# Moving the down projection's operand and the channel-form operand to other places modulo 512 bytes

## The chip, the core and the metric

The kernel runs on one core of one Trainium2 chip. The metric is the device time of one execution in microseconds (us), lower is better; the median of the runs shown is taken. TensorE (PE) multiplies, its weight loads are listed apart as PEld, VectorE is DVE, ScalarE is ACT, GpSimd is POOL, SyncE is SP.

## What is computed

Twelve layers on 256 tokens of 1024 channels, all in float32: RWKV-7 mixing, attention, two gated short convolutions, a neighbourhood attention, a Hyena mixer, and after each of these six mixers a gated feed-forward network (FFN). Cut to what matters here:

```python
def swiglu(h, w13, w2):                       # the FFN, w2 is the down projection, 2816 x 1024
    g, u = jnp.split(h @ w13, 2, axis=-1)
    return (jax.nn.silu(g) * u) @ w2

def short_conv_mixer(h, w_in, conv_w, w_out): # layers 4 and 10
    b_gate, c_gate, u = jnp.split(h @ w_in, 3, axis=-1)
    return (b_gate * depthwise_conv3(c_gate * u, conv_w)) @ w_out

def hyena_mixer(h, w_in, short_w, ..., w_out): # layer 8
    v, x1, x2 = jnp.split(depthwise_conv3(h @ w_in, short_w, short_b), 3, axis=-1)
    ...                                        # two long convolutions by Fourier transforms
    return z @ w_out

for i in range(DEPTH_2):                       # and a first block of four layers before it
    x = x + mixer(rmsnorm(x, norm_mix_g[i]))
    x = x + swiglu(rmsnorm(x, norm_ffn_g[i]), f_w13[i], f_w2[i])
```

## The kernel before

Every large product is made from three products of rounded numbers. A float32 weight w is split into w_hi (rounded to the type float32r, by ACT, line 1232) and w_lo (the rest, by DVE, line 1666); the activations likewise into a hi and a lo half. `PE_PASSES = ((0, 0), (0, 1), (1, 0))` then gives hi by hi, hi by lo and lo by hi, so three matmuls follow each other for each piece of work, and each loads a stationary operand of its own.

The weights stream in as quarters of 128 x 1024 elements (512 KB) through four slots of `w_raw`, are split into `w_hi` and `w_lo` or, in the layers that have room for them, also into `w_hi_extra` and `w_lo_extra`. A matmul comes in two forms:

- **Token form** (`part_tokens`, line 391; `project`, line 495; `project_part`, line 978): 128 columns of the activations are loaded as the stationary operand, and 512 columns of a weight quarter are streamed past them (the moving operand). The FFN's down projection is `project` on the tiles `hidden_hi` and `hidden_lo` (HH and HL in the code), of 22 blocks of 256 elements a partition.
- **Channel form** (`block_channels`, line 464): 128 columns of a weight quarter are the stationary operand, and the 256 tokens of the activations in `operand_hi` and `operand_lo` (`ah`, `al`) are streamed. It stands in the input projections of the layers 4, 8 and 10 only.

The moving operand of one matmul is read while the stationary operand of the next one is loaded: in the trace of layer 4 the load for the next matmul starts in the same hundredth of a us as the matmul itself.

A place in SBUF is counted in bytes within a partition. From the order of the declarations follow the places of all tiles. Modulo 512, `w_hi`, `w_lo`, `w_hi_extra`, `w_lo_extra`, `operand_hi`, `operand_lo`, `hidden_hi`, `hidden_lo`, `conv_hi` and `conv_lo` all stand at 128 (a tile `align_phases` of 32 bytes sees to that for the last ones), and every block that a matmul takes from them starts a multiple of 512 bytes further on. So with all matmuls of the two forms both operands start at the same place modulo 512; the text calls the difference between them the distance, and it is 0. Two kinds of matmul have another one. In the neighbourhood attention (layer 6) the lines 939 and 941 load `ident_r`, which stands at 256, and stream 256 columns of `bias_hi` or `bias_lo`, at 128: their distance is 128 bytes (float32r, as in the two forms). In layer 0 the line 531 loads columns of `l1_rw` (shown as `l_rw`), whose eight blocks lie 1152 bytes apart, and streams 256 columns of `tmp_rw` blocks 1024 bytes apart: distances of 0, 128, 256 and 384 in turn (plain float32).

ACT writes `operand_hi` (line 1244) and DVE `operand_lo` (line 1687) from PSUM when a layer starts, in four halves of 128 x 512; the channel form's first matmul waits for them. The order of the work is written out by hand, engine by engine. Hyena's own output projection takes `operand_hi` and `operand_lo` too, in token form, after its channel-form products.

Of the kernel before, what the change touches and what calls it, by code (L numbers as in the profile page):

```python
# [37 lines left out]
FK = FF // P  # L38
FB = FF // 256
SLOTS = 4  # L40
QW = 1024
# [17 lines left out]
ORDER, BANDS, FHID = 2, 16, 64  # L59
# [4 lines left out]
LAYER_NORMS = 4  # L64
# [31 lines left out]
def program(nc, A, out, layers=LAYERS):  # L96
# [3 lines left out]
    def keep(name, shape, dtype=F32):  # L100
        return ctx.enter_context(nc.sbuf_tensor(name, shape, dtype))
# [13 lines left out]
    wlo = keep("w_lo", [P, SLOTS, QW], F32R)  # L115
    [ART] = scope(("ar_turned", [P, 2, KT, SEQ]))
    [RHS] = scope(("rhs_rw", [P, TT, 2, KT, HD]))
    ah, al = keep("operand_hi", [P, KT, SEQ], F32R), keep("operand_lo", [P, KT, SEQ], F32R)
    tok = keep("token_scratch", [P, TT, D])
    ident = keep("ident_sb", [P, P])  # L120
    identb = keep("identb_sb", [P, P], BF16)
# [13 lines left out]
    with ExitStack() as s:  # L135
# [37 lines left out]
    XT, XX = IC[:].rearrange("p t (k n) -> p (t k) n", n=SEQ), DEC[:].rearrange("p t (k n) -> p (t k) n", n=SEQ)  # L173
    MIX = [TMP[:].rearrange("p t (k n) -> p (t k) n", n=SEQ), KK[:].rearrange("p t (k n) -> p (t k) n", n=SEQ)]

    HH, HL, SILU, HM, FIRSTG = scope(
        ("hidden_hi", [P, FK, SEQ], F32R), ("hidden_lo", [P, FK, SEQ], F32R),
        ("silu_ff", [P, 2, TT, 256]), ("hidden_ff", [P, 2, TT, 256]), ("first_rms_gain", [P, D]))
    [*_, xhi, xlo] = scope(("ff_below", [P, 2 * FK * SEQ + 4 * TT * 256 + D]), ("w_hi_extra", [P, SLOTS, QW], F32R), ("w_lo_extra", [P, SLOTS, QW], F32R))

    with ExitStack() as s:
        def attend(name, shape, dtype=F32):
            return s.enter_context(nc.sbuf_tensor(name, shape, dtype))

        QTOK, KTOK, VTOK = attend("q_at", [P, TT, D]), attend("k_at", [P, TT, D]), attend("v_at", [P, TT, D])
        QT, KTT2 = attend("q_turned", [P, KT, SEQ]), attend("k_turned_at", [P, KT, SEQ])
        PR, PT = attend("probs_at", [P, 2, TT, 2, SEQ]), attend("probs_turned", [P, 2, TT, SEQ])
        ROT = attend("rot_at", [P, TT, 512])
        BIASH = attend("bias_hi", [P, HEADS, BIAS_W], F32R)
        attend("extra_rest", [P, 2 * SLOTS * QW - HEADS * BIAS_W])  # L190
        [BIAS] = scope(("bias_at", [P, HEADS, BIAS_W]))
        [BIASL] = scope(("bias_lo", [P, HEADS, BIAS_W], F32R))
        attend("bias_both", [P, HEADS, BIAS_W])
        SUMS, NMAX, RSUM = attend("sums_at", [P, TT, HEADS]), attend("nmax_at", [P, TT, HEADS]), attend("rsum_at", [P, TT, HEADS])
        ROPE, CAUSAL, CSTAGE = attend("rope_sb", [P, TT, 2, 2, HD]), attend("causal_sb", [P, P], BF16), attend("causal_stage", [P, P])
        QG, BMASK, IDR = attend("qk_gain", [P, 3, HD]), attend("bias_mask", [P, GRID_W]), attend("ident_r", [P, P], F32R)
    OH, OL, CT, ZT, CV, YT = scope(
        ("conv_hi", [P, KT, SEQ], F32R), ("conv_lo", [P, KT, SEQ], F32R), ("c_conv", [P, KT, SEQ]),
        ("z_conv", [P, KT, SEQ]), ("conv_out", [P, KT, SEQ]), ("y_conv", [P, KT, SEQ]))
    HV, HX1, HX2, HF, EO2, FR, WIN, SKIP, STAGE, HT, DFTP, DTMP, EMBT, FW, FW3, TAPS3, FCOL, H1, ARG, ONES, COL, SGN, NCOL, SEAM, HALF = scope(  # L200
        ("v_hy", [P, TT, D]), ("x1_hy", [P, TT, D]), ("x2_hy", [P, TT, D]), ("filter_freq", [P, 4, D]),
        ("even_odd2", [P, 4, D]), ("taps_or_freq", [P, 4, D]), ("window_sb", [P, TT, D]), ("skip_sb", [P, ORDER, D]),
        ("dft_stage", [P, 4, 2, P]), ("dft_sb", [P, 6, P]), ("dft_parity", [P, 2, 2, P]), ("dft_tmp", [P, 2, P]),
        ("emb_sb", [EMB, SEQ]), ("f_w12", [FHID, 2, P]), ("f_w3_sb", [P, ORDER, D]), ("taps3_sb", [P, 4, 3 * KT]),
        ("f_cols", [P, 3]), ("hid_hy", [P, SEQ]), ("arg_hy", [P, 2, SEQ]), ("ones_sb", [P, P]), ("half_angles", [P, 8, 4]),
# [134 lines left out]
    def weight(w, q):  # L340

        return W[w][bank(q)][:, q % SLOTS, :]
# [40 lines left out]
    def _(pe):  # L383
# [64 lines left out]
                    elif k in (5, 7):  # L448
                        turn_half(src, 1, k // 7)

        def block_channels(q, pair, operand_waits=False, after={}):


            for i in range(4):
                s = (q + i) % SLOTS
                if operand_waits and i % 2 == 0:
                    pe.wait_ge(m["operand_ready"], due(m["operand_ready"], 3 if i == 0 else 1))
                pe.wait_ge(w_lo[s], nth(q + i))
                for kk in range(2):
                    kt = 2 * i + kk  # L460
                    for c in range(4):
                        for x, w in PE_PASSES:

                            mm = pe.matmul(acc[:, 2 * pair + c // 2, (c % 2) * SEQ:(c % 2 + 1) * SEQ],  # L464
                                           weight(w, q + i)[:, kk * 512 + c * P:kk * 512 + (c + 1) * P], (ah, al)[x][:, kt, :],
                                           start=(kt == 0 and c % 2 == 0 and (x, w) == (0, 0)),
                                           stop=(kt == KT - 1 and c % 2 == 1 and (x, w) == (1, 0)), skip_group_check=True)
                mm.then_inc(w_used[s], 1)
                if i in after:
                    after[i]()  # L470
# [576 lines left out]
        def conv(q, first):  # L1047
            if first:
                keep_busy(7)
            turn(tok, 0, halves=True)  # L1050
            keep_busy(2 if first else 3)
            turn(tok, 1, halves=True)
            keep_busy(2 if first else 1, bank=0)
            for j in range(6):
                if j >= 2:
                    freed = m["c_done"] if j < 4 else m["z_done"]
                    pe.wait_ge(freed, due(freed))
                block_channels(q + 4 * j, j % 2, operand_waits=(j == 0))
            ready = lambda: pe.wait_ge(m["conv_lo_done"], due(m["conv_lo_done"]))
            read = lambda: pe.wait_ge(m["y_done"], due(m["y_done"], 2))  # L1060
            project(q + IN_Q, KT, OH, OL, {(0, 0): ready, (0, 1): read, (4, 0): ready}, near_end=tok, held=6)


        def hyena(q):
# [137 lines left out]
            pe.wait_ge(m["ones_set"], due(m["ones_set"]))  # L1202
            pe.wait_ge(m["dft_built"], due(m["dft_built"]))
            for j in range(6):
                block_channels(q + 4 * j, j % 2, operand_waits=(j == 0), after={i: lambda i=i: inside_block(j, i) for i in range(4)})
            free(m["dft_done"])
            dft(1, 3)
            free(m["freq_done"])
# [14 lines left out]
    def _(act):  # L1223
# [13 lines left out]
                if q + k + SLOTS < quarters:  # L1237
                    split(q + k + SLOTS, at)

        def operand(t):  # L1240

            for h in range(2):
                act.wait_ge(m["turned"], due(m["turned"]))
                act.activation(ah[:, 4 * h:4 * h + 4, t * P:(t + 1) * P], aux[:, 2 * t + h, :].rearrange("p (k n) -> p k n", n=P), ACT.Copy)\
                   .then_inc(m["hi_ready"], 1)

        def both_operands():
            for t in range(TT):
                operand(t)

        def residual(n, q):

# [54 lines left out]
            if channels:  # L1307
                if n >= LAYER_NORMS:
                    ahead(q - 4, 1)
                ahead(q - 3, 1)  # L1310
                square(1)
                both_operands()
                ahead(q - 2, 2)
                return
            ahead(q - 4, 1)
# [343 lines left out]
    def _(dve):  # L1659
# [19 lines left out]
            instruction.then_inc(m["dve_step"], 1)  # L1679
            dve.wait_ge(m["dve_step"], due(m["dve_step"]))  # L1680

        def operand(t, halves=(0, 1)):

            for h in halves:
                dve.wait_ge(m["hi_ready"], due(m["hi_ready"]))
                own = (slice(None), slice(4 * h, 4 * h + 4), slice(t * P, (t + 1) * P))
                dve.tensor_tensor(al[own], aux[:, 2 * t + h, :].rearrange("p (k n) -> p k n", n=P), ah[own].bitcast(F32), ALU.subtract)\  # L1687
                   .then_inc(m["operand_ready"], 1)

        def both_operands():  # L1690
            for t in range(TT):
                operand(t)

        def wide(v, shape, axis):
            return v.unsqueeze(axis).to_broadcast(shape)
# [4 lines left out]
        def residual(n, q):  # L1700
# [57 lines left out]
            if layer_norm and rms:  # L1758
                add_with_stats(0, 0)
                add_with_stats(0, 1)  # L1760
                moments(0)
                centred(0)
                ahead(q - 4, 1)
                normed(0)
                add_with_stats(1, 0)
                add_with_stats(1, 1)
                moments(1)
                centred(1)
                normed(1)
                rms_normed(0)  # L1770
                rms_normed(1)
                both_operands()
                ahead(q - 3, 3)
                return
            if layer_norm:
# [68 lines left out]
            if channels:  # L1844
                add(1, 1)
                rms_normed(1)
                both_operands()
# [1040 lines left out]
```

## Time and profile before

| | |
|---|---|
| runs shown | 2018.6, 2013.73, 2016.08 us |
| median | 2016.08 us |
| profiled execution, time | 2017.66 us |
| profiled execution, span (first to last instruction) | 2015.8 us |
| mean granted TensorE clock | 0.995 |
| PE busy | 1969.3 us (98%) |
| PEld busy | 1612.0 us (80%) |
| DVE busy | 1264.4 us (63%) |
| ACT busy | 890.4 us (44%) |

The span is the time from the first to the last instruction; 1.9 us of the execution's time lie around it. A matmul's recorded duration is longer than the time it adds, because matmuls are pipelined: the next one starts long before the recorded end. What counts below is the pitch, the time from the start of one matmul to the start of the next.

### The profile page before, as it was taken

How to read it: one execution, taken by the hardware profiler on the slowest of the kernel's cores; microseconds unless marked ns; L12 is line 12 of the kernel's file. 1: busy time of each engine (PE TensorE's matmuls, PEld its weight loads, DVE VectorE, ACT ScalarE, POOL GpSimd, SP SyncE). 2: the span in 40 equal slices, each digit the busy share in tenths (PEclk: the TensorE clock that was granted, in tenths of full speed). 3: DMA queues.
4: the chain of work that ended last, by engine and by line, in shares of the span. 5: the costliest groups of instructions: out<-in, count | busy, mean ns of one | idle time of the engine just before them, and what ended most of it. 6: DMA issues, size and time to landing. Idle time of an engine off the chain costs nothing.

```text
span 2015.8 us, 32431 instructions
## 1 busy us (share of the span) xinstructions
PE 1969.3 (98%) x12730; PEld 1612.0 (80%) x12730; DVE 1264.4 (63%) x1623; ACT 890.4 (44%) x1282; POOL 168.5 (8%) x198
## 2 busy tenths in 40 slices
PE   7999999999999999999999999999999999999999
PEld 5689788887688879888878678877767888898887
DVE  7875854576764566655757655567986554576543
ACT  4552353444543434443545544434434444435442
POOL 1243100000010010000012021001100000000000
PEclk9999999999999999999999999999999999999999
DMA  8411365644266645655455157553224556455544
GB/s 292 130 48 62 125 207 195 208 169 157 97 213 212 192 140 202 209 184 195 159 183 178 64 178 234 195 183 126 105 74 147 197 178 218 145 181 187 190 162 149
DMA packets 93047, 336.04 MB, mean 167 GB/s; under 512 B 11230, under 2 KB 11364, under 8 KB 92623
## 3 DMA queue, kind: packets, MB, share of 16 engines
q1 hardware_dynamic: 85824, 311.62, 45.4%
q0 software_dynamic: 7120, 22.95, 4.0%
q8 instruction: 77, 1.26, 0.3%
q14 instruction: 26, 0.21, 0.0%
HBM read 332.43 MB, written 1.05 MB: 165 GB/s over the span
## 4 chain that ended last, share of the span: by engine, by line
PE 88%; DVE 7%; issue 1%; POOL 1%; ACT 1%; DMA 0%; SPq 0%; DVEq 0%; POOLq 0%; ACTq 0%
PE acc L391 42%; PE acc L495 21%; PE acc L464 9%; PE acc L978 2%; DVE w_lo L1666 1%; PE aux L895 1%; PE aux L934 1%; PE aux L679 1%; DVE w_lo_extra L1666 1%; POOL rstd L2548 1%; PE aux L966 1%; PE aux L955 1%; PE aux L514 0%; DVE operand_lo L1687 0%; PE aux L879 0%
## 5 line engine op out<-in xcount | busy, mean ns | idle before, releaser
L1666 DVE TENSOR_TENSOR w_lo<-w_raw,w_hi 128x1024 fp32r<-128x1024 f32 x376 | 450.5, 1222 | 180.7 <-ACT w_hi L1232 175.9
L1232 ACT ACTIVATE w_hi<-w_raw 128x1024 fp32r<-128x1024 f32 x376 | 388.3, 1057 | 306.3 <-PE acc L391 108.7
L391 PE MATMUL acc<-w_hi,operand_hi 128*128 128x512 f32 x848 | 338.8, 400 | 15.8 <-DVE operand_lo L1880 12.1
L391 PE MATMUL acc<-w_hi,operand_lo 128*128 128x512 f32 x848 | 332.8, 392 | 0.0
L391 PE MATMUL acc<-w_lo,operand_hi 128*128 128x512 f32 x848 | 332.3, 392 | 0.0
L1666 DVE TENSOR_TENSOR w_lo_extra<-w_raw,w_hi_extra 128x1024 fp32r<-128x1024 f32 x212 | 251.6, 1221 | 50.0 <-ACT w_hi_extra L1232 45.7
L1232 ACT ACTIVATE w_hi_extra<-w_raw 128x1024 fp32r<-128x1024 f32 x212 | 215.7, 1058 | 82.3 <-DMA w_raw<-in_weights 67.6
L2103 DVE TENSOR_TENSOR hidden_ff<-silu_ff,acc 128x256 f32<-128x256 f32 x132 | 49.5, 417 | 251.6 <-ACT silu_ff L1450 251.6
L391 PEld LDWEIGHTS acc<-w_hi,operand_hi 128*128 128x128 f32 x848 | 160.3, 189 | 50.5 <-DVE operand_lo L1880 11.9
L391 PE MATMUL acc<-w_hi_extra,operand_hi 128*128 128x512 f32 x496 | 196.1, 395 | 1.1 <-DVE w_lo_extra L1666 0.8
L391 PE MATMUL acc<-w_hi_extra,operand_lo 128*128 128x512 f32 x496 | 193.5, 390 | 0.0
L391 PE MATMUL acc<-w_lo_extra,operand_hi 128*128 128x512 f32 x496 | 193.2, 390 | 0.0
L391 PEld LDWEIGHTS acc<-w_hi,operand_lo 128*128 128x128 f32 x848 | 160.0, 189 | 34.2
L391 PEld LDWEIGHTS acc<-w_lo,operand_hi 128*128 128x128 f32 x848 | 160.4, 189 | 32.2 <-issue 0.5
L1450 ACT ACTIVATE silu_ff<-acc 128x256 f32<-128x256 f32 x132 | 43.3, 379 | 300.2 <-PE acc L391 300.1
L495 PE MATMUL acc<-w_hi,hidden_hi 128*128 128x512 f32 x352 | 138.4, 393 | 0.0
L495 PE MATMUL acc<-w_hi,hidden_lo 128*128 128x512 f32 x352 | 137.2, 390 | 0.0
L495 PE MATMUL acc<-w_lo,hidden_hi 128*128 128x512 f32 x352 | 137.0, 389 | 0.0
L464 PE MATMUL acc<-operand_hi,w_hi 128*128 128x256 f32 x384 | 115.7, 301 | 0.8 <-DVE operand_lo L1687 0.8
L391 PEld LDWEIGHTS acc<-w_hi_extra,operand_hi 128*128 128x128 f32 x496 | 93.1, 188 | 21.8 <-DVE w_lo_extra L1666 2.5
L464 PE MATMUL acc<-operand_hi,w_lo 128*128 128x256 f32 x384 | 109.1, 284 | 0.0
L464 PE MATMUL acc<-operand_lo,w_hi 128*128 128x256 f32 x384 | 109.0, 284 | 0.0
(516 smaller groups left out, 3240.6 us busy)
## 6 DMA issues: line engine op xcount, KB each, us to landing
w_raw<-in_weights SPq DMA_DIRECT2D x588, 512.0 KB, 4.5
ln_gain<-in_gains POOLq DMA_DIRECT2D x7, 512.0 KB, 4.5
bias_at<-in_rpb POOLq DMA_DIRECT2D x12, 256.0 KB, 6.2
ln_gain<-in_ln_g POOLq DMA_DIRECT2D x4, 512.0 KB, 4.6
ln_bias<-in_ln_b POOLq DMA_DIRECT2D x4, 512.0 KB, 6.2
vec_rw<-in_vec POOLq DMA_DIRECT2D x3, 512.0 KB, 4.8
l_rw<-in_lora SPq DMA_DIRECT2D x1, 1152.0 KB, 10.4
iclr_rw<-in_xT SPq DMA_DIRECT2D x2, 512.0 KB, 4.5
```

What stands on the lines that cost most here:

```text
L391: mm = pe.matmul(acc[:, 2 * pair + t, :], (ah, al)[x][:, kt, t * P:(t + 1) * P], weight(w, q + i)[:, kk * 512:(kk + 1) * 512], start=(kt = ...
L464: mm = pe.matmul(acc[:, 2 * pair + c // 2, (c % 2) * SEQ:(c % 2 + 1) * SEQ], weight(w, q + i)[:, kk * 512 + c * P:kk * 512 + (c + 1) * P], ...
L495: mm = pe.matmul(acc[:, 2 * t + c, :], (hi, lo)[x][:, kt, t * P:(t + 1) * P], weight(w, q + kt)[:, c * 512:(c + 1) * 512], start=(kt == 0 ...
L679: mm = pe.matmul(ps(4 + u % 2)[half_of(1 - s), kt * CH:(kt + 1) * CH], NM[of, u // 2, u % 2, kt, :], INVT[of, u // 2, u % 2, kt, :], start ...
L895: mm = pe.transpose(aux[:, odd, kk * SEQ + t * P:kk * SEQ + (t + 1) * P], HM[:, odd, t, kk * P:(kk + 1) * P], ident[:])
L934: mm = pe.matmul(aux[:, h, t * SEQ:t * SEQ + keys], QT[of, p, t * P:(t + 1) * P], KTT2[of, p, 0:keys], start=True, stop=False, skip_group_ ...
L955: mm = pe.transpose(aux[:, 2 + h, k * SEQ + t * P:k * SEQ + (t + 1) * P], PR[:, p % 2, t, h, k * P:(k + 1) * P], ident[:])
L978: mm = pe.matmul(acc[:, 2 * t + c, :], (ah, al)[x][:, kt, t * P:(t + 1) * P], weight(w, q + IN_Q + kt)[:, c * 512:(c + 1) * 512], start=(k ...
L1232: act.activation(weight(0, q), raw[:, s, :], ACT.Copy).then_inc(w_hi[s], 1)
L1450: last = act.activation(SILU[:, odd, t, :], acc[:, 2 * pair + t, 0:256], ACT.Silu)
L1666: dve.tensor_tensor(weight(1, q), raw[:, s, :], weight(0, q).bitcast(F32), ALU.subtract).then_inc(w_lo[s], 1)
L2103: dve.tensor_tensor(HM[:, odd, t, :], SILU[:, odd, t, :], acc[:, 2 * pair + t, 256:512], ALU.mult).then_inc(m["hidden_ready"], 1)
```

## The change

The instructions and their order on all five engines are the same before and after; only places in SBUF differ.

- Padding shifts tiles up. `hidden_hi` then stands at 384 modulo 512 and `hidden_lo` at 0. With the streamed weights at 128, the down projection's stationary operand has the distances 256 (hi) and 384 (lo) in place of 0.
- `operand_hi` and `operand_lo` are declared 128 elements (512 bytes) longer. Everywhere but in the channel form they are used from their start, as before. In the channel form of layer n, ACT and DVE write them, and PE streams them, from `places[n]` elements on: distances from the weights of 256 (hi) and 320 (lo) bytes in layer 4, 384 and 448 in layer 8, 160 and 32 in layer 10.
- The FFN's `silu_ff`, `hidden_ff` and `first_rms_gain` come to 0 modulo 512 from 128. All other tiles keep their place modulo 512 (they move by 1024 or 1536 bytes).

```diff
-    ah, al = keep("operand_hi", [P, KT, SEQ], F32R), keep("operand_lo", [P, KT, SEQ], F32R)
+    rooms = [keep(n, [P, KT * SEQ + 128], F32R) for n in ("operand_hi", "operand_lo")]
+    ah, al = [x[:, 0:KT * SEQ].rearrange("p (k n) -> p k n", n=SEQ) for x in rooms]
+    places = {4: (64, 80), 8: (96, 112), 10: (40, 8)}
+    by_channel = {n: [x[:, at:at + KT * SEQ].rearrange("p (k n) -> p k n", n=SEQ) for x, at in zip(rooms, places[n])] for n in places}
...
-    HH, HL, SILU, HM, FIRSTG = scope(
-        ("hidden_hi", [P, FK, SEQ], F32R), ("hidden_lo", [P, FK, SEQ], F32R),
+    _, HH, _, HL, SILU, HM, FIRSTG = scope(
+        ("below_hidden_hi", [P, 64]), ("hidden_hi", [P, FK, SEQ], F32R),
+        ("below_hidden_lo", [P, 32]), ("hidden_lo", [P, FK, SEQ], F32R),
         ("silu_ff", [P, 2, TT, 256]), ("hidden_ff", [P, 2, TT, 256]), ("first_rms_gain", [P, D]))
-    [*_, xhi, xlo] = scope(("ff_below", [P, 2 * FK * SEQ + 4 * TT * 256 + D]), ("w_hi_extra", [P, SLOTS, QW], F32R), ("w_lo_extra", [P, SLOTS, QW], F32R))
+    [*_, xhi, xlo] = scope(("ff_below", [P, 2 * FK * SEQ + 4 * TT * 256 + D + 128]), ("w_hi_extra", [P, SLOTS, QW], F32R), ("w_lo_extra", [P, SLOTS, QW], F32R))
...
+        attend("below_extra", [P, 128])
         BIASH = attend("bias_hi", [P, HEADS, BIAS_W], F32R)
...
-        def block_channels(q, pair, operand_waits=False, after={}):
+        def block_channels(q, pair, n, operand_waits=False, after={}):
...
                             mm = pe.matmul(acc[:, 2 * pair + c // 2, (c % 2) * SEQ:(c % 2 + 1) * SEQ],
-                                           weight(w, q + i)[:, kk * 512 + c * P:kk * 512 + (c + 1) * P], (ah, al)[x][:, kt, :],
+                                           weight(w, q + i)[:, kk * 512 + c * P:kk * 512 + (c + 1) * P], by_channel[n][x][:, kt, :],
...
-        def operand(t, halves=(0, 1)):
+        def operand(t, halves=(0, 1), hi=ah, lo=al):
...
-                dve.tensor_tensor(al[own], aux[:, 2 * t + h, :].rearrange("p (k n) -> p k n", n=P), ah[own].bitcast(F32), ALU.subtract)\
+                dve.tensor_tensor(lo[own], aux[:, 2 * t + h, :].rearrange("p (k n) -> p k n", n=P), hi[own].bitcast(F32), ALU.subtract)\
                    .then_inc(m["operand_ready"], 1)

-        def both_operands():
+        def channel_operands(n):
             for t in range(TT):
-                operand(t)
+                operand(t, hi=by_channel[n][0], lo=by_channel[n][1])
```

## Rows read from the trace of the kernel before

**Rows 1.** The page: busy time of each engine, then the chain that ended last.
```profile
PE 1969.3 (98%) x12730; PEld 1612.0 (80%) x12730; DVE 1264.4 (63%) x1623; ACT 890.4 (44%) x1282; POOL 168.5 (8%) x198
...
PE 88%; DVE 7%; issue 1%; POOL 1%; ACT 1%; DMA 0%; SPq 0%; DVEq 0%; POOLq 0%; ACTq 0%
```

**Rows 2.** Groups by line: engine, op, out<-in, shape, count | busy us, mean ns | idle before.
```profile
L495 PE MATMUL acc<-w_hi,hidden_hi 128*128 128x512 f32 x352 | 138.4, 393 | 0.0
...
L464 PE MATMUL acc<-operand_hi,w_hi 128*128 128x256 f32 x384 | 115.7, 301 | 0.8 <-DVE operand_lo L1687 0.8
...
L495 PE MATMUL acc<-w_hi_extra,hidden_hi 128*128 128x512 f32 x176 | 69.3, 394 | 0.0
...
L464 PE MATMUL acc<-operand_hi,w_hi_extra 128*128 128x256 f32 x192 | 54.7, 285 | 0.0
```

**Rows 3.** Chain in order of time, last down projection: start us, us, what and count.
```profile
1958.19 54.47 PE acc L495 x240
```

**Rows 4.** The same chain view over layer 4's channel form.
```profile
753.06 68.98 PE acc L464 x575
```

**Rows 5.** Stretches: us, PE busy (instructions touching it), granted clock, DMA share, GB/s.
```profile
760.00:800.00 40.00, 40.00 (x336) 1.00 0.59 196
1960.00:2000.00 40.00, 40.00 (x178) 1.00 0.53 184
```

**Rows 6.** Plain float32 at lines 1098 and 531: PE timeline, and groups by line.
```profile
1495.79 3.60 PE L1098 MATMUL aux<-v_hy,dft_sb 128*128 128x512 f32 x8
...
36.43 3.40 PE L531 MATMUL aux<-tmp_rw,l_rw 128*64 128x256 f32 x15
...
L1098 PE MATMUL aux<-v_hy,dft_sb 128*128 128x512 f32 x32 | 15.0, 595 | 0.6 <-DVE taps_or_freq L2438 0.6
...
L531 PE MATMUL aux<-tmp_rw,l_rw 128*64 128x256 f32 x32 | 7.3, 382 | 0.0
```

**Rows 7.** PE timeline, layer 6: bias matmuls at distance 128, one pair of heads.
```profile
1106.07 0.39 PE L939 MATMUL aux<-bias_hi,ident_r 128*128 128x256 f32 x1
1106.30 0.28 PE L941 MATMUL aux<-bias_lo,ident_r 128*128 128x256 f32 x1
1106.41 0.28 PE L939 MATMUL aux<-bias_hi,ident_r 128*128 128x256 f32 x1
1106.54 0.28 PE L941 MATMUL aux<-bias_lo,ident_r 128*128 128x256 f32 x1
...
1107.60 0.29 PE L941 MATMUL aux<-bias_lo,ident_r 128*128 128x256 f32 x1
1107.72 0.28 PE L939 MATMUL aux<-bias_hi,ident_r 128*128 128x256 f32 x1
1107.84 0.29 PE L941 MATMUL aux<-bias_lo,ident_r 128*128 128x256 f32 x1
```

**Rows 8.** PE timeline, token form at distance 0, just after float32 matmuls.
```profile
485.27 0.39 PE L391 MATMUL acc<-w_lo_extra,operand_hi 128*128 128x512 f32 x1
485.50 0.40 PE L391 MATMUL acc<-w_hi_extra,operand_lo 128*128 128x512 f32 x1
485.74 0.40 PE L391 MATMUL acc<-w_hi_extra,operand_hi 128*128 128x512 f32 x1
485.97 0.39 PE L391 MATMUL acc<-w_lo_extra,operand_hi 128*128 128x512 f32 x1
486.19 0.39 PE L391 MATMUL acc<-w_hi_extra,operand_lo 128*128 128x512 f32 x1
...
487.58 0.39 PE L391 MATMUL acc<-w_hi_extra,operand_lo 128*128 128x512 f32 x1
```

**Rows 9.** PE timeline, channel form at distance 0, just after float32 matmuls.
```profile
1386.84 0.28 PE L464 MATMUL acc<-operand_hi,w_lo 128*128 128x256 f32 x1
1386.95 0.29 PE L464 MATMUL acc<-operand_lo,w_hi 128*128 128x256 f32 x1
1387.08 0.28 PE L464 MATMUL acc<-operand_hi,w_hi 128*128 128x256 f32 x1
1387.19 0.28 PE L464 MATMUL acc<-operand_hi,w_lo 128*128 128x256 f32 x1
```

**Rows 10.** Groups by line, DVE and ACT: who writes what the change moves.
```profile
L2103 DVE TENSOR_TENSOR hidden_ff<-silu_ff,acc 128x256 f32<-128x256 f32 x132 | 49.5, 417 | 251.6 <-ACT silu_ff L1450 251.6
L2107 DVE TENSOR_TENSOR hidden_lo<-aux,hidden_hi 128x512 f32 (+1 forms) x66 | 45.1, 684 | 26.4 <-ACT hidden_hi L1455 26.4
L1687 DVE TENSOR_TENSOR operand_lo<-aux,operand_hi 128x512 fp32r<-128x512 f32 x52 | 34.5, 686 | 36.4 <-ACT operand_hi L1244 36.1
```

More of the change, by code:

```diff
@@ L199, in program @@
         ("z_conv", [P, KT, SEQ]), ("conv_out", [P, KT, SEQ]), ("y_conv", [P, KT, SEQ]))
-    HV, HX1, HX2, HF, EO2, FR, WIN, SKIP, STAGE, HT, DFTP, DTMP, EMBT, FW, FW3, TAPS3, FCOL, H1, ARG, ONES, COL, SGN, NCOL, SEAM, HALF = scope(
+    HV, HX1, HX2, HF, _, EO2, FR, WIN, SKIP, STAGE, HT, DFTP, DTMP, EMBT, FW, FW3, TAPS3, FCOL, H1, ARG, ONES, COL, SGN, NCOL, SEAM, HALF = scope(
         ("v_hy", [P, TT, D]), ("x1_hy", [P, TT, D]), ("x2_hy", [P, TT, D]), ("filter_freq", [P, 4, D]),
-        ("even_odd2", [P, 4, D]), ("taps_or_freq", [P, 4, D]), ("window_sb", [P, TT, D]), ("skip_sb", [P, ORDER, D]),
+        ("below_even_odd2", [P, 128]), ("even_odd2", [P, 4, D]), ("taps_or_freq", [P, 4, D]), ("window_sb", [P, TT, D]), ("skip_sb", [P, ORDER, D]),
         ("dft_stage", [P, 4, 2, P]), ("dft_sb", [P, 6, P]), ("dft_parity", [P, 2, 2, P]), ("dft_tmp", [P, 2, P]),
@@ L1057, in conv @@
                     pe.wait_ge(freed, due(freed))
-                block_channels(q + 4 * j, j % 2, operand_waits=(j == 0))
+                block_channels(q + 4 * j, j % 2, LAYER_NORMS if first else 10, operand_waits=(j == 0))
             ready = lambda: pe.wait_ge(m["conv_lo_done"], due(m["conv_lo_done"]))
@@ L1204, in hyena @@
             for j in range(6):
-                block_channels(q + 4 * j, j % 2, operand_waits=(j == 0), after={i: lambda i=i: inside_block(j, i) for i in range(4)})
+                block_channels(q + 4 * j, j % 2, 8, operand_waits=(j == 0), after={i: lambda i=i: inside_block(j, i) for i in range(4)})
             free(m["dft_done"])
@@ L1238, in ahead, with operand @@
                     split(q + k + SLOTS, at)
-        def operand(t):
+        def operand(t, hi=ah):
             for h in range(2):
                 act.wait_ge(m["turned"], due(m["turned"]))
-                act.activation(ah[:, 4 * h:4 * h + 4, t * P:(t + 1) * P], aux[:, 2 * t + h, :].rearrange("p (k n) -> p k n", n=P), ACT.Copy)\
+                act.activation(hi[:, 4 * h:4 * h + 4, t * P:(t + 1) * P], aux[:, 2 * t + h, :].rearrange("p (k n) -> p k n", n=P), ACT.Copy)\
                    .then_inc(m["hi_ready"], 1)
-        def both_operands():
+        def channel_operands(n):
             for t in range(TT):
-                operand(t)
+                operand(t, by_channel[n][0])
         def residual(n, q):
@@ L1311, in residual @@
                 square(1)
-                both_operands()
+                channel_operands(n + 1)
                 ahead(q - 2, 2)
@@ L1686, in operand, with channel_operands @@
                 own = (slice(None), slice(4 * h, 4 * h + 4), slice(t * P, (t + 1) * P))
-                dve.tensor_tensor(al[own], aux[:, 2 * t + h, :].rearrange("p (k n) -> p k n", n=P), ah[own].bitcast(F32), ALU.subtract)\
+                dve.tensor_tensor(lo[own], aux[:, 2 * t + h, :].rearrange("p (k n) -> p k n", n=P), hi[own].bitcast(F32), ALU.subtract)\
                    .then_inc(m["operand_ready"], 1)
-        def both_operands():
+        def channel_operands(n):
             for t in range(TT):
-                operand(t)
+                operand(t, hi=by_channel[n][0], lo=by_channel[n][1])
         def wide(v, shape, axis):
@@ L1771, in residual @@
                 rms_normed(1)
-                both_operands()
+                channel_operands(n + 1)
                 ahead(q - 3, 3)
@@ L1846, in residual @@
                 rms_normed(1)
-                both_operands()
+                channel_operands(n + 1)
                 ahead(q - 3, 3)
```

## The prediction

> **What bounds the kernel now.** The page first: PE is busy for 98% of the span and 88% of the chain that ended last is PE's, with DVE at 7% [rows 1]. A busy share near 100% does not yet say how fast the matmuls go, because their recorded durations overlap. So the pitch comes next. The chain over the last down projection is one piece, 240 matmuls in 54.47 us, 227.0 ns each [rows 3]. In a stretch of 40 us of it, 178 instructions touch the stretch; each is recorded as 0.39 long, so (40.00 + 0.39) / 178 = 226.9 ns [rows 5]. Layer 4's channel form is one piece too: 575 matmuls in 68.98 us, 120.0 ns each [rows 4], and 336 in a stretch of 40 us, (40.00 + 0.28) / 336 = 119.9 ns [rows 5]. The granted clock in both is 1.00, the 2.4 GHz level, at which 512 columns take 213.3 ns and 256 take 106.7. Both forms thus pay the same 13.3 ns on top of their columns. The reader is to see that in these two places nothing waits for data: every nanosecond of pitch is a nanosecond of the time, and nothing but the pitch is.
>
> How much pitch the change touches [rows 2]: the down projection is 3 passes of 352 and 3 of 176 matmuls, 1584; the channel form 3 of 384 and 3 of 192, 1728. So **one nanosecond more or less** is worth 1.58 us in the first, 1.73 us in the second, 3.3 us in both, against a time of 2016. I call less than 0.2% (4.0 us) no change; that is about what a measurement of this kernel can tell, the three runs themselves lying 4.9 us apart. A mean pitch change of 1.2 ns over the 3312 matmuls is the border.
>
> **What the change removes and adds.** No instruction is added, removed or moved on any engine, and no wait or DMA. What differs is which bytes of a partition are read together. In a group of three passes the matmul hi by w_hi streams while hi is loaded again, hi by w_lo while lo is loaded, lo by w_hi while the next hi is loaded. So in the down projection two matmuls in three run at distance 256 and one at 384. In the channel form the streamed half counts: two in three at 256, 384 or 160 bytes (layers 4, 8, 10) and one in three at 320, 448 or 32. All had 0.
>
> The trace of before has no long run of float32r matmuls at another distance, so the price of the new ones must be bounded by neighbours.
>
> The nearest row is layer 6's bias: float32r, 256 columns, a stationary operand loaded for each matmul, at a distance of 128 bytes. From 1106.30 to 1106.54 are two pitches, 120 ns each; for the next 128 queries, from 1107.60 to 1107.84, again two of 120 ns [rows 7]. That is the channel form's 120.0 at distance 0 to within the rounding of 5 ns a pitch. It is the only direct sight of another distance, and it shows none of an effect. Its weakness: these runs are four matmuls long, right behind plain float32 matmuls.
>
> The next row is plain float32 at line 531, where 0, 128, 256 and 384 follow each other: fifteen matmuls in 3.40 us, the last recorded as 0.38, so 3.02 / 14 = 216 ns at every one of the four distances [rows 6]. Two of them are the ones the down projection gets. Plain float32 takes two cycles a column (213.3 ns for 256), so it reads its moving operand at half the rate; a conflict could hide there.
>
> I take **zero** for both terms, by the bias row, which is nearest in type, size and rate. Sum: 1584 x 0 + 1728 x 0 = 0.
>
> The Trainium skill, page "SBUF — State Buffer", section "Who interferes with whom", speaks for the same value: TensorE has two SBUF read ports that are independent, one for the moving operand and one for the weight load, and it never waits for anybody. By that rule no distance can matter. It does not explain the 13.3 ns, though, and the rows below say why I do not lean on it.
>
> **The bounds.** One thing in the trace shows that the pitch is not a constant of the shape. After plain float32 matmuls the token form, still at distance 0, goes through steps of 0.23, 0.24, 0.23 and 0.22 us; ten pitches from 485.27 to 487.58 are 231 ns in the mean [rows 8], and only then it settles at 226.9. The channel form, likewise, steps by 0.11, 0.13 and 0.11, 117 ns in the mean [rows 9], before it settles at 120. So something between the load and the stream, at equal places, is worth from -7 to +13 ns in the token form (0.22 to 0.24) and from -10 to +10 in the channel form (0.11 to 0.13). If the new distances held the matmuls at those ends for good, the down projection would move by -11 to +21 us and the channel form by -17 to +17. These are the outer bounds from rows of the same type: 1988 to 2054. That the start has such steps at all is the reason why I give "no change" only about half of the chance.
>
> **Smaller terms.** `silu_ff`, `hidden_ff` and the hidden halves change their place for DVE and ACT. The 132 products into `hidden_ff` take 417 ns each and had idled 251.6 us for their input, the 66 of `hidden_lo` take 684 [rows 10]. They run beside PE's gate and up products, and PE shows no idle time before the down projection [rows 2]; zero, and if they were 10% slower still zero. The channel operands are on the path: 4 writes a layer of 686 ns on DVE [rows 10], PE idle 0.8 us in all for them at line 464 [rows 2]. If their new places made them 10% slower, 12 x 0.07 = 0.8 us at the very most. No other tile changes its place modulo 512. DMA into `w_raw` lands where it did, modulo 512.
>
> **Rivals.**
>
> *Slower: the token form never settles.* The quiet 226.9 would be a locked state that equal places allow: load and stream start together, at the same place, and repeat. At 256 and 384, alternating in every group of three, they would stay in the unsettled steps of rows 8 at 231 ns, 4.1 ns more: 1584 x 4.1 = 6.5 us. For the channel form unsettled steps lie at or below 120, so I charge nothing: 2016.1 + 6.5 = 2022.6. For it speaks that the steps of rows 8 vary with nothing but the recent past; against it that the bias row at distance 128 shows the settled value within three matmuls. It decides as soon as the down projection's pitch is above 229.5 ns. At 0.24 us and 0.13 us it would be the upper bound.
>
> *Faster: the 13.3 ns are a conflict of equal places.* Plain float32 at line 1098 has 512 columns and new weights for each matmul: (3.60 - 0.59) / 7 = 430 ns for 426.7 ns of columns, 3 ns over; line 531 is 216 for 213.3 [rows 6]. The float32r forms pay about 10.5 ns more than that. If both reads beginning at the same place caused it, and every new distance were free of it, the change would save 3312 x 10.5 = 35 us: 1981. If only one of the two halves of each operand were free of it (one in three or two in three matmuls), 12 to 23 us: 1993 to 2004. For it speaks that the excess is the same 13.3 ns in both forms, as a collision in a load of the same size would be; against it that distance 128 pays it too [rows 7].
> The Trainium skill, page "TensorE: Matmul & The Clock Gate", section "Wait — 56ns, not 53.3ns?", gives columns / 2.4 + about 2.5 ns for back-to-back matmuls, 215.8 and 109.2 ns. The trace disagrees for float32r with a load each time (226.9 and 120.0). By that rule, were it reached, the saving would be 1584 x 11.1 + 1728 x 10.8 = 36 us.
>
> *A mixture.* With eight distances, some may cost and some may save, and the sum may fall anywhere in between; this widens the range on both sides and adds no value of its own. That the change does not do what it says can be left out: the places follow from the declarations.
>
> **How the numbers follow.** No effect of distance, 0.5: 2016.1, the median of before, since the profiled execution (2017.66, span 2015.8 and 1.9 around it) lies 1.6 above that median and nothing is added to it. Slower, 0.27: 2022.6 and up to some 2035. Faster, 0.23: a partial case, 1993 to 2011, has 0.17 of it, the full one, 1981, 0.06. Even without an effect three runs may miss the border by chance, about one time in twenty on each side, which comes out of the 0.5. So: faster 0.24, same 0.47, slower 0.29. The range leaves out the full gain and most of the half one (0.1) and the top of the slower case (0.07): 2003 to 2030. If there is no effect, its own range is 2012 to 2020.
>
> **What would show it.** In the changed trace the chain piece of the last down projection, 240 matmuls in 54.5 us if I am right, 55.4 if they never settle, 52 if the excess goes; and in its steady stretch whether the passes of hi (256) and of lo (384) differ from each other. Layers 4, 8 and 10 each give the channel pitch at two distances, to be read as start-to-start steps that repeat in threes: 120, 120, 120 if I am right. The first gate and up products keep distance 0 and must stay at 227 in every case; if they move, the cause is not the distance. The forecast is wrong if any of the eight distances settles more than 4 ns from 227 or 120.

## The result

The changed kernel takes 2021.3 us in the median of 8 runs, against 2015.95 us for the kernel before in as many: a ratio of 1.0021, with a 95% interval from 1.0011 to 1.0030. It is slower by some 5 us: 0.21% by the ratio, a hair over the 0.2% that the prediction called no change, and inside its range. Its likeliest case, no effect at all, is not what happened.

The page of the changed kernel, busy times; they answer to [rows 1]:

```profile
PE 1974.3 (98%) x12730; PEld 1612.4 (80%) x12730; DVE 1264.7 (63%) x1623; ACT 890.4 (44%) x1282; POOL 167.9 (8%) x198
```

PE is busy 5.0 us longer with the same 12730 matmuls; the other engines are where they were. The span went from 2015.8 to 2020.9 us. The chain of the changed kernel, the last down projection and the channel forms of the layers 4 and 10 (start, us, what, count), answers to [rows 3, 4]. `project` is now line 500, `block_channels` line 469:

```profile
1962.23 55.50 PE acc L500 x240
```
```profile
757.03 69.10 PE acc L469 x576
```
```profile
1739.61 68.43 PE acc L469 x576
```

The down projection's 240 matmuls take 55.50 us where they took 54.47: 231.3 ns each for 227.0. The channel form of layer 4 has not moved (69.11 us for its 576 before), that of layer 10 has become faster by 0.94 us (69.37 before):

```profile
753.06 69.11 PE acc L464 x576
...
1734.73 69.37 PE acc L464 x576
```

Those two rows are of the kernel before. The groups by line show where in a group of three passes the time went. Of the changed kernel, then of the one before (mean ns of one is the number behind the comma):

```profile
L500 PE MATMUL acc<-w_hi,hidden_lo 128*128 128x512 f32 x352 | 139.7, 397 | 0.0
L500 PE MATMUL acc<-w_lo,hidden_hi 128*128 128x512 f32 x352 | 139.3, 396 | 0.0
L500 PE MATMUL acc<-w_hi,hidden_hi 128*128 128x512 f32 x352 | 138.3, 393 | 0.0
```
```profile
L495 PE MATMUL acc<-w_hi,hidden_lo 128*128 128x512 f32 x352 | 137.2, 390 | 0.0
L495 PE MATMUL acc<-w_lo,hidden_hi 128*128 128x512 f32 x352 | 137.0, 389 | 0.0
```

Two passes of three cost 7 ns more, the third (393 in [rows 2] as well) nothing. These are recorded durations, in whole ns; their mean, of 7, 7 and 0, is 4.7. The steps from start to start say 4.1.

**The ledger.** The mean step from start to start over the whole stretch (steps over 260 ns left out) rose in the six down projections by 4.06, 4.20, 4.08, 2.95, 4.20 and 4.19 ns; times 264 matmuls each, +6.25 us. In the channel forms it changed by 0.0 (layer 4), -0.55 (layer 8) and -1.64 ns (layer 10), times 575, 553 and 575 steps, -1.25 us. Together +5.0 us, against +5.1 between the two spans and +5.3 between the medians. These are two single executions, and the executions of one kernel lie up to 5 us apart, so the close agreement is partly luck; but the steps leave no room for another cause inside the moved stretches. The token form whose distance did not change kept its steps: 227.5 and 227.6 ns in the mean at line 391 (now 396), 230.2 and 230.4 at line 978 (now 983).

DVE's and ACT's smaller terms are nil, as forecast; of the changed kernel, to be held against [rows 10]:

```profile
L2108 DVE TENSOR_TENSOR hidden_ff<-silu_ff,acc 128x256 f32<-128x256 f32 x132 | 49.6, 417 | 251.5 <-ACT silu_ff L1455 251.5
L2112 DVE TENSOR_TENSOR hidden_lo<-aux,hidden_hi 128x512 f32 (+1 forms) x66 | 45.2, 684 | 26.9 <-ACT hidden_hi L1460 26.9
L1692 DVE TENSOR_TENSOR operand_lo<-aux,operand_hi 128x512 fp32r<-128x512 f32 x52 | 34.5, 686 | 35.7 <-ACT operand_hi L1249 35.5
```

### The profile page after: what moved, and what is told of

Read it like the earlier page. It is cut to its first block, busy times and chain, and to the rows that moved or that the text cites. A ratio compares the mean times of both kernels' runs of the same rounds, so it can differ in the third digit from the quotient of the medians.

```text
span 2020.9 us, 32431 instructions
## 1 busy us (share of the span) xinstructions
PE 1974.3 (98%) x12730; PEld 1612.4 (80%) x12730; DVE 1264.7 (63%) x1623; ACT 890.4 (44%) x1282; POOL 167.9 (8%) x198
## 4 chain that ended last, share of the span: by engine, by line
PE 88%; DVE 7%; issue 1%; POOL 1%; ACT 1%; DMA 0%; SPq 0%; DVEq 0%; POOLq 0%; ACTq 0%
PE acc L396 42%; PE acc L500 21%; PE acc L469 9%; PE acc L983 2%; DVE w_lo L1671 2%; PE aux L900 1%; PE aux L684 1%; PE aux L939 1%; POOL rstd L2553 1%; DVE w_lo_extra L1671 1%; PE aux L971 1%; PE aux L960 1%; DVE operand_lo L1692 0%; PE aux L519 0%; PE aux L1081 0%
## 5 line engine op out<-in xcount | busy, mean ns | idle before, releaser
L396 PEld LDWEIGHTS acc<-w_hi_extra,operand_lo 128*128 128x128 f32 x496 | 93.1, 188 | 19.9
```

Of the source, the lines that this page charges most:

```text
L396: mm = pe.matmul(acc[:, 2 * pair + t, :], (ah, al)[x][:, kt, t * P:(t + 1) * P], weight(w, q + i)[:, kk * 512:(kk + 1) * 512], start=(kt = ...
```

## The experiments

All experiments are the changed kernel with other places; none changes an instruction or what is computed. In all of them the weights stay at 128 modulo 512 and one operand moves: the one that is loaded in the token form, the one that is streamed in the channel form. So the runs show what the place of that operand costs beside weights at 128. Whether it is the distance between the two reads that counts, or the place of the moved operand by itself, none of them separates; "distance" below is a name for the place, counted from the weights'.

For the down projection each FFN got places of its own, in elements of 4 bytes (these are same_distance's):

```diff
+    [HH_ROOM] = scope(("hidden_hi", [P, FK * SEQ + 128], F32R))
+    _, HL_ROOM = scope(("below_hidden_lo", [P, FK * SEQ]), ("hidden_lo", [P, FK * SEQ + 128], F32R))
+    hidden_places = {1: (16, 16), 3: (32, 32), 5: (64, 64), 7: (96, 96), 9: (8, 8), 11: (4, 4)}
+    HIDDEN = {n: [x[:, at:at + FK * SEQ].rearrange("p (k n) -> p k n", n=SEQ) for x, at in zip((HH_ROOM, HL_ROOM), hidden_places[n])] for n in hidden_places}
```

with `silu_ff` and what follows it back at 128 modulo 512. Below, a pair as (256, 384) gives the distances of hi and lo in bytes. Pitches of the down projection are the length of its last chain piece by its count (216 to 240 matmuls); layer 7 has other matmuls in between and is read from single steps. In the kernels with this edit `project` is line 502 and `block_channels` line 471. The six kernels that try many distances (same_distance, lo_alone, more_same, more_lo, channel_a, channel_b) were executed once each, and only their steps are used, not their times.

### Each half alone

```diff
-    places = {4: (64, 80), 8: (96, 112), 10: (40, 8)}
+    places = {4: (0, 0), 8: (0, 0), 10: (0, 0)}
```

> The changed kernel with the channel form put back to distance 0, so the down projection alone is moved (hi 256, lo 384). In the trace of the changed kernel the down projection's pitch is 231.1 ns in the mean where it was 227.0, 1584 x 4.1 = 6.5 us, and the channel forms save 1.2 us. If the distances are the whole cause: pitch 231.1 again, channel 120.0, time 6 to 7 us above the kernel before, 1 us above the changed one. If instead something else that moved (silu_ff, hidden_ff, the shift of all tiles by 1024 bytes) is the cause, both forms keep what the changed kernel shows.

Measured: 2021.79 us against 2017.43, ratio 1.0021 (1.0011 to 1.0031). The pitch is the changed kernel's to the last digit:

```profile
1963.60 55.50 PE acc L500 x240
```

The other half, `hidden_places` all (0, 128) elements, which is distance 0, and the channel form as in the change:

> The changed kernel with the down projection put back to distance 0 (silu_ff and hidden_ff back at 128 too) and the channel form at the six distances of the change. If the distances are the whole cause: down projection 227.0 ns, channel form 120.0, about 119.2 and 118.3 ns in the layers 4, 8 and 10 as in the changed kernel, time 1 us below the kernel before, which a timing can't tell from none. If the two parts act on each other, the sum of this kernel's difference and of only_down's is not the changed kernel's +5.

Measured: 2015.54 us against 2017.43, ratio 0.9994 (0.9984 to 1.0003), no difference that can be told. The down projection is back at 54.47 us for 240. Layer 10 repeats its 68.42 us. But layer 4, at the same two distances as in the changed kernel, does not:

```profile
752.46 67.84 PE acc L471 x576
```

67.84 us in place of 69.10, 117.8 ns in place of 120.0. In the changed kernel the steps there repeat as 117, 121, 122 ns; here as 118, 118, 118, 117, 118, 118, 117, 119, 117. Both patterns hold from the tenth matmul to the last. So one and the same pair of distances has two steady states. Layer 8, where the channel form runs in pieces of 24 matmuls between others, shows them side by side: at (384, 448) 12 of 23 pieces of the changed kernel settle at 117.8 ns and the others at 120.0 to 121.2, within one execution, where all pieces of the kernel before settle at 120.0. What picks one of them, no run here shows.

The sum of the halves by the trace, +6.3 and -2.6 us, is not quite the change's +5.0, and it is this layer 4 that makes up the difference.

### Is it the distance, or the change between two distances?

The prediction's slower rival said that alternating places keep the matmuls from settling. Hi and lo at one distance take the alternation away:

> Hi and lo at one and the same distance, another one in each FFN: 64, 128, 256, 384, 32 and 16 bytes in the layers 1, 3, 5, 7, 9 and 11; channel form 256, 128 and 64 bytes in the layers 4, 8 and 10. Theory one, it is the change between two distances that keeps the matmuls from settling: every stretch settles at 226.7 (token) and 120.0 ns (channel), as at distance 0. Theory two, each distance has a price of its own: the pitch at 256 is about 231, at 384 about 232 to 234, and others differ from 226.7; the channel form at 256 about 117 to 121.

And lo alone moved, hi left at 0:

> Hi at distance 0, lo at another: 16, 32, 64, 128, 256 and 384 bytes in the layers 1, 3, 5, 7, 9 and 11; channel form lo at 256, 128 and 64 bytes in the layers 4, 8 and 10. Theory one, the change between two distances costs: the mean pitch is above 227 in the down projections, most where the step between hi and lo is a certain one (128 in the change), and the pitch repeats in threes. Theory two, each distance has a price of its own: of three matmuls the one during which lo is loaded departs from 226.7, the other two don't, so a mean of a third of that distance's price.

The down projections of same_distance, layers 1 (64 bytes), 3 (128), 5 (256), 9 (32) and 11 (16):

```profile
369.08 53.20 PE acc L502 x228
```
```profile
685.55 50.41 PE acc L502 x216
```
```profile
979.79 53.15 PE acc L502 x234
```
```profile
1675.58 50.42 PE acc L502 x216
```
```profile
1959.76 54.42 PE acc L502 x240
```

233.3, 233.4, 227.1, 233.4 and 226.8 ns. Theory one falls: without any alternation, 64, 128 and 32 bytes cost 6.4 ns a matmul, more than the change's mixture, and 256 and 16 cost nothing. The distance itself has a price, and 256 has that of 0. Of lo_alone, layers 9 (lo at 256) and 11 (lo at 384):

```profile
1677.90 49.03 PE acc L502 x216
```
```profile
1960.66 55.50 PE acc L502 x240
```

227.0 and 231.3 ns. (0, 384) gives the very 55.50 us of the change's (256, 384), which is the same pair modulo 256.

But theory two in its simple form falls too. (0, 16) takes 232.2 ns though 0 and 16 alone take 227, and (0, 128) spreads its cost over two matmuls of three (steps of 227, 233 and 234 in layer 7, 231.0 in the mean) though lo is loaded beside one of them only. A mixture has a price of its own.

### More distances

> Hi and lo at one distance: 8, 48, 96, 160, 240 and 4 bytes in the FFNs of the layers 1, 3, 5, 7, 9 and 11; channel form both at 32 (layer 4), both at 16 (layer 8), hi 0 and lo 16 (layer 10). If the pitch depends on the distance modulo 256 and steps by halves of 13.3 ns: 226.7 or 233.3 ns in every stretch, 160 and 96 at 233.3. If there is a distance free of the 13.3 ns, it would show as 213 to 220 here.

> Hi and lo apart: (0, 8), (0, 48), (16, 256), (0, 240), (0, 96) and (128, 256) bytes in the FFNs of the layers 1, 3, 5, 7, 9 and 11; channel form (0, 96), (0, 32) and (0, 32) in the layers 4, 8 and 10. If only the distance modulo 256 counts, (128, 256) is a changed order of the change's own (256, 384): two matmuls in three at 128 and one at 0. Where each matmul pays for the load beside it alone: 231.1 with two in three at 233.3. Where a matmul pays for a load at 128 either beside it or just before it: all three at 233.3.

The pair (128, 256) of more_lo, and both at 8 bytes and both at 4 of more_same:

```profile
1961.91 56.02 PE acc L502 x240
```
```profile
370.61 52.60 PE acc L502 x228
```
```profile
1959.91 55.78 PE acc L502 x240
```

233.4, 230.7 and 232.4 ns. In (128, 256) hi lies at 128 and lo at 0 (modulo 256), and the steps behind the three passes are 233, 232 and 235 ns in turn, as the third of the expectations had it: a matmul pays when the load beside it, or the one just before, is at the dear distance. The change's order, hi at 0 and lo at 128, has one pass in three with neither, and that is the one that stayed at 227. That rule fits these two pairs; (0, 16) shows that it is not the whole.

The steps of a half of 13.3 ns (226.7 or 233.3) which were expected do not hold everywhere: 4, 8, 24 and 240 bytes lie between, at 232.4, 230.7, 231.1 and 228.5, and 96 above, at 234.2.

### Does the period of 256 hold, and does a distance repeat?

> Token form, hi and lo at one distance: 272, 320, 496, 12 and 20 bytes in the layers 1, 3, 5, 9 and 11, and hi 256 with lo 0 in layer 7. Channel form both at 96, 160 and 48 in the layers 4, 8 and 10. If only the distance modulo 256 counts: 226.7 ns at 272 as at 16, 233.3 at 320 as at 64, 228.3 at 496 as at 240, 226.7 for 256 with 0 (plus what layer 7's matmuls in between add, 228 in before). If the period is 512, 272 and 320 differ from 16 and 64. Below 226.7: nowhere, if the 13.3 ns are not a matter of places.

> Distances seen before, now in other layers: token form both at 16, 8, 128 and 64 bytes in the layers 3 (and 7), 5, 9 and 11, which showed 226.7, 230.7, 233.3 and 233.3 in the layers 11, 1, 3 and 1; 24 bytes is new. Channel form both at 224, 96 and 192 in the layers 4, 8 and 10. If a distance alone sets the pitch, each repeats within 0.2 ns; if a stretch can settle in more than one way, one of them comes out otherwise.

Of channel_a, both at 272 and both at 320; of channel_b, both at 16 and both at 128:

```profile
371.11 51.69 PE acc L502 x228
```
```profile
686.07 50.41 PE acc L502 x216
```
```profile
688.49 48.98 PE acc L502 x216
```
```profile
1675.43 50.41 PE acc L502 x216
```

226.7 at 272 as at 16, 233.4 at 320 as at 64, and 228.2 at 496 as 228.5 at 240: the place counts modulo 256 bytes, not 512. In the last pieces of the layers 1, 3, 5, 9 and 11 every distance with hi and lo alike that was tried in two layers repeated within 0.2 ns.

Layer 7 did not. channel_b has both at 16 bytes there too, and two of its pieces, with the same 48 matmuls at the same distance, are:

```profile
1314.88 11.38 PE acc L502 x48
1326.89 11.08 PE acc L502 x48
```

The first settles into steps of 233, 234, 231, 234, 235, 233 (233.3 in the mean), the second into 227, 227, 226 (226.7). Of the five pieces of 24 to 48 matmuls, two settle the first way and three the second. The last 60 begin the second way, and from one late step (250 ns) on they go the first way. At distance 0, in the kernel before, every piece settles at 226.7, and so do the last 60 on both sides of a late step (247 ns). So the second of channel_b's expectations came true: the token form too has two steady states, and 16 bytes, unlike 0, can fall into the dear one.

What the last pieces of the down projection showed:

| distance, bytes | ns a matmul |
|---|---|
| both 0, 16, 256, 272 | 227.0, 226.8, 227.1, 226.7 |
| both 240, 496 | 228.5, 228.2 |
| both 8, 24 | 230.7, 231.1 |
| both 4, 12, 20 | 232.4, 233.4, 233.4 |
| both 32, 48, 64, 128, 320 | 233.3 to 233.4 |
| both 96 | 234.2 |
| (0, 256) | 227.0 |
| (0, 8), (0, 64), (0, 384), (256, 384) | 231.1 to 231.3 |
| (0, 16), (0, 48), (0, 96), (16, 256) | 232.2, 232.3, 232.6, 232.5 |
| (0, 32), (128, 256) | 233.4 |

Layer 7 adds, where its pieces settle: both 160, 233.3 ns; both 384, 231.7 to 233.3; (0, 128), 231.1; (256, 0), 226.7 as at 0; (0, 240) likewise, but 231 after the late step. No distance tried is below that of 0. The faster rival, that equal places cause the 13.3 ns over the columns, has no support in the token form. The 192 bytes that turn out best in the channel form below were not tried here. There it is the streamed operand that lies 192 above the loaded one; counted the other way that is 64, modulo 256, and 64 is dear here.

### Does the price belong to every token-form matmul?

```diff
-    ah, al = [x[:, 0:KT * SEQ].rearrange("p (k n) -> p k n", n=SEQ) for x in rooms]
+    ah, al = [x[:, 32:32 + KT * SEQ].rearrange("p (k n) -> p k n", n=SEQ) for x in rooms]
```

> Hi and lo of operand_hi and operand_lo at distance 128 wherever the token form uses them (lines 391, 495 and 978 of before: 4032 + 192 + 192 = 4416 matmuls); down projection and channel form at distance 0. Of the 128-byte distance the down projection of layer 3 showed 233.3 ns against 226.7. If that price belongs to every token-form matmul, whatever the layer: 4416 x 6.7 = 29 us more than the kernel before, about 2046. If it belongs to the down projection's layout alone, the time stays at 2016 to 2018.

Measured: 2038.39 us against 2018.11, ratio 1.0099 (1.0082 to 1.0116), 20 us more. A block of 48 matmuls, of this kernel and then of the one before:

```profile
254.47 11.20 PE acc L398 x48
```
```profile
250.70 10.91 PE acc L391 x48
```

233.3 against 227.3 ns. The price is the token form's at large, not the down projection's. It comes to less than the 29 us expected: the mean step over all these stretches rose by 5.4 ns, not by 6.7, which makes 24 us, and the spans differ by 22.6. Part of the reason is that the steps after plain float32 matmuls are near 231 already [rows 8]. It is also the plainest proof that places matter: 1% of the kernel by moving one operand 128 bytes.

The price has a condition that the trace of token_128 shows. Here, at the same 128 bytes, the granted clock is 0.50, the 1.2 GHz level (first the stretch, with the clock behind the count, then two of its matmuls, five steps apart):

```profile
1049.50:1052.30 2.80, 2.80 (x8) 0.50 0.75 246
1049.44 0.63 PE L398 MATMUL acc<-w_hi,operand_hi 128*128 128x512 f32 x1
1051.57 0.63 PE L398 MATMUL acc<-w_hi,operand_lo 128*128 128x512 f32 x1
```

2.13 us for five steps are 426 ns each, and 512 columns at 1.2 GHz take 426.7: neither the 20.0 nor the 13.3 ns are there. The channel form steps by 213 to 214 ns at that level, 256 columns at 1.2 GHz, in the kernel before as in channel_192. So in these traces both the excess over the columns and what places do to it show at 2.4 GHz only.

### The channel form

There the distance helps. All three layers at (0, 64), at 32 and at 192 bytes; the edit of the last (places in elements of 4 bytes):

```diff
-    places = {4: (64, 80), 8: (96, 112), 10: (40, 8)}
+    places = {4: (48, 48), 8: (48, 48), 10: (48, 48)}
```

> Down projection at distance 0, channel form with hi at 0 and lo at 64 bytes in all three layers. Layer 10 showed 117.8 ns there against 120.0. If all three layers settle so: 1728 x 2.2 = 3.8 us less than the kernel before, 2012. If a stretch can settle in two ways (layer 4 showed 120.0 in the changed kernel and 117.8 in only_channel at the very same distances), one or two of the layers stay at 120.0 and less than 3 us is gained.

> Down projection at distance 0; channel form with hi and lo both at 32 bytes in the layers 4, 8 and 10. Layer 4 showed 116.7 ns there against 120.0. If that is what 32 bytes give in every layer: 1728 x 3.3 = 5.7 us less than the kernel before, about 0.3%. If the value depends on how a stretch begins, one layer stays near 119 to 120 and 4 us or less is gained.

> Down projection at distance 0; channel form with hi and lo both at 192 bytes in the layers 4, 8 and 10. Layer 10 showed 113.3 ns there against 120.0, the lowest pitch of any distance tried. If that is what 192 bytes give in every layer: 1728 x 6.7 = 11.5 us less than the kernel before, about 0.57%, 2006 us. If the state depends on how a stretch begins, layer 4 or 8 stays near 118 to 120 and the gain is 4 to 8 us.

The layers 4 and 10 of channel_lo64, then of channel_192:

```profile
757.85 69.11 PE acc L471 x576
```
```profile
1739.42 68.11 PE acc L471 x576
```
```profile
753.01 65.30 PE acc L471 x576
```
```profile
1728.45 65.57 PE acc L471 x576
```

| | layer 4 | layer 8 | layer 10 | median, of before | ratio (interval) |
|---|---|---|---|---|---|
| channel_lo64 | 120.0 | 118.6 | 117.8 | 2013.69, 2018.11 | 0.9980 (0.9969 to 0.9990) |
| channel_32 | 116.7 | 117.0 | 116.7 | 2012.83, 2017.82 | 0.9976 (0.9967 to 0.9985) |
| channel_192 | 113.4 | 115.4 | 113.4 | 2009.66, 2017.72 | 0.9963 (0.9949 to 0.9977) |

(Mean steps in ns; before has 120.0, 119.7 and 120.0.) channel_192 is faster than the kernel before, by 8 us in the medians and 10 in the spans (2005.7 for 2015.8), and its slowest run (2015.63) lies below the changed kernel's fastest (2019.0). Its steps are 113, 113, 114 ns from the eighth matmul on: 6.7 ns over the 106.7 of the columns instead of 13.3. In layer 8, where other matmuls come in between every 24, each piece takes some five steps to settle, and then 14 of the 21 pieces that can be read settle at 113.3 ns and 7 at 117.8. The sum by steps is 10.0 us (3.8, 2.4 and 3.8) where 11.5 was expected. channel_32 met the first of its expectations: 5.3 us by its steps and 5.0 in the medians, where 5.7 was expected.

channel_lo64 met the second of its expectations: layer 4 at 120.0 and layer 10 at 117.8 at the same distances. By its steps it should gain 1.9 us; the runs say 4.4, with 2.0 at the interval's edge. The profiled execution was the slowest of the eight (2021.1 us): its first down projection comes to its long last piece at 374.96 us, the kernel before's at 370.24, ahead of anything that differs in its distances. So an execution can gain or lose some 5 us elsewhere, and a gain of 2 us is not to be read from times like these. Whether layer 4 settles at 117.8 in the executions that were not profiled is open.

Other distances gave, in the layers 4 or 10: both 48 or both 224, 118.3; both 64, 117.8; both 96 and both 256, 120.0; (0, 16) 118.9; (0, 32) 117.1; (0, 96) 117.8.

## Why the prediction was right or wrong

**The bound and the price of a nanosecond: right.** The pitch was the time: 6.25 - 1.25 us counted in steps gave the 5.1 us of the spans, at 1.58 us a nanosecond for the down projection.

**Zero for both terms: wrong.** This is the step that failed, the prediction's "I take zero for both terms, by the bias row". The term 1584 x 0 measured +6.25 us, the term 1728 x 0 -1.25. It rested on the bias rows [rows 7], called nearest in type, size and rate. They are nearest in size to the channel form and not to the down projection: at 128 bytes a 256-column matmul is at 119 to 120 ns (layer 8 of same_distance has 118.9 in the mean), while a 512-column one costs 6.4 ns more. So the row was right about its own shape and was carried to another one. Whether it is the number of columns that makes the difference, no run separates from the other one, that the loaded operand moves in the token form and the streamed one in the channel form. Rounding to 10 ns a step and runs of four matmuls could in any case not have shown the 2 or 3 ns by which the channel form's distances differ.

**The plain float32 row was rightly doubted.** Its 216 ns at all four distances [rows 6] stand, and float32r has its full price at 128. The caution written beside it, that another rate may hide a conflict, was the right one. The bias row got a caution as well, for its short runs, but none for its 256 columns. The prediction's own sign of being wrong was met: the steps at the dear passes settle at 232 and 234 ns, more than 4 from 227.

**The slower rival: right in its price, half right in its mechanism.** It gave 231 ns, 6.5 us and 55.4 us for the last piece; measured were 231.1 ns in the mean, 6.25 us and 55.50 us. But the matmuls do settle, into a pattern of three (227, 232, 234), and most of the price is that of the distance 128 (modulo 256) itself, which costs 233.4 when nothing alternates. That (256, 384) came out at the 231 of the unsettled steps looks like luck: it is two passes of three at some 6.7 over 226.7. Where alternation has its own price, as in (0, 16), the rival's mechanism is there too.

**The faster rival: wrong where it was aimed, right in a corner.** No distance tried took the token form below 226.7. The channel form at 192 lost half of its 13.3 ns. The change's own six distances, at 117.8 to 120, missed it.

**The bounds were sound.** 220 to 240 and 110 to 130 ns, from the steps after plain float32 [rows 8, 9], hold the mean pitch of every stretch in the changed kernel and the twelve experiments, and these steps were what gave the rivals half of the chance against a row that seemed to say zero.

**The rule of the Trainium skill** on TensorE's two independent read ports (page "SBUF — State Buffer", "Who interferes with whom"), that it never waits for anybody, was read in the prediction as "no distance can matter". The prediction rightly did not lean on that, for it is wrong: in token_128 nothing changed but the place of one operand, and the pitch rose from 227.3 to 233.3 ns. Whether the load and the stream hinder each other, against the rule, or the moved read by itself is slower at some places, these runs do not tell: the weights never moved.

## What to carry to other kernels

When a stretch is bound by the pitch of matmuls that each load new weights, look at the step from start to start against columns by 2.4 GHz; if there is something over, try the places of the two operands modulo 256 bytes, separately for each shape, since the best distance tried for 512 columns with the loaded operand moved (0) was not that for 256 columns with the streamed one moved (192). Give the parts of a split operand, hi and lo, the same place: (0, 16) cost 232.2 ns where 0 and 16 alone cost 227. A row prices only the shape that it has: a neighbour with half the columns said zero where the truth at 128 bytes was 3%.

## What the runs showed of the hardware

- float32r matmuls with a load each settle, with both halves alike, mostly at 13.3 or 20.0 ns over their columns in the token form (226.7, 233.3; 4, 8, 24, 240 and 96 bytes gave 228.5 to 234.2) and at 6.7, 10.0, 11.1, 11.7 or 13.3 in the channel form (113.3, 116.7, 117.8, 118.3, 120.0). At 0 bytes both forms have 13.3. What in the chip makes these steps, no run here tells.
- At a granted clock of 0.50 there is no excess: 427 ns for 512 columns at distances 0 and 128 (before, token_128), 213 for 256 at 0 and 192 (before, channel_192).
- With the weights' place fixed, that of the other operand counts modulo 256 bytes (0 as 256, 16 as 272, 64 as 320, 240 as 496). 16 bytes can be as good as 0 (layers 3 and 11, and 272 in layer 1), which 8 and 24 never were, but it can also fall to 233.3 (layer 7 of channel_b).
- A stretch can have two steady states at the same distances: layer 4 at (256, 320) with 120.0 or 117.8 ns in two kernels, layers 4 and 10 at (0, 64) in one execution, pieces of layer 7 at 16 bytes with 226.7 or 233.3, pieces of layer 8 at 192 bytes with 113.3 or 117.8. At distance 0 every stretch read settled in one way only (226.7, 120.0). What picks a state was not tried.
